# Mixers' recurrence: the pairwise key-query products in column quarters and halves of TensorE

## The chip, the cores and the metric

The kernel runs on one core of a Trainium2 chip. The metric is the device time of one execution in microseconds; lower is better. The profile is that of one profiled execution.

## The reference, cut to what matters

The program is a block with four mixers and experts, and behind it a block of two hybrid layers. The change lies in the hybrid layers, in the gated recurrence that runs over the sequence once forwards and once backwards:

```python
def hgrn2_chunk_scan(q, k, v, g):
    ...
        diff = bt[:, :, :, None, :] - bt[:, :, None, :, :]
        dec = jnp.where(mask, jnp.exp(jnp.where(mask, diff, 0.0)), 0.0)
        attn = jnp.einsum('bhtk,bhtsk->bhts', qt, dec * kt[:, :, None, :, :])
        o_intra = jnp.einsum('bhts,bhsv->bhtv', attn, vt)
...
    g_f = hgrn_log_forget(...)
    g_b = hgrn_log_forget(...)
    o_fwd = hgrn2_chunk_scan(hq, -jnp.expm1(g_f), hv, g_f)
    o_bwd = jnp.flip(hgrn2_chunk_scan(jnp.flip(hq, 1), jnp.flip(-jnp.expm1(g_b), 1),
                                      jnp.flip(hv, 1), jnp.flip(g_b, 1)), 1)
```

There are 512 tokens, four heads of width 128 and two layers. For each pair of a query token t and a key token s not behind it, `attn` is a sum over 128 channels of query times key times the decay between the two.

## The kernel before

**Tiling.** In the kernel a chunk is 128 tokens, so there are four chunks (`NT`) and four heads (`H`). The decay between s and t has no form that is safe over 128 tokens in one product, so `attn` of a chunk is put together in six rounds. `round0` makes the pairs that lie within the same four tokens. `level(d, i)`, with i from 1 to 5, makes the pairs that lie in the two halves of a block of 8, 16, 32, 64 and 128 tokens: in each block one half holds the queries, the other the keys (`half_of(i)` is 4, 8, 16, 32, 64). `d` is 0 for the forward direction and 1 for the backward one.

**Before the change** each of these products is made for all 128 keys of a chunk at once: 16 products in a round (four chunks, four heads), each with a 128x128 operand of keys as weights and with 128 query columns (`round0`) or 64 (`level`) as input. The result, 128 keys by the queries, goes to PSUM (`L`, named `lev` in the rows, four banks). Most of it is of no use, since a key of one block is never paired with a query of another. VectorE then copies only the wanted pairs under a mask into `att` (`keep0`, `keep`: L3865 and L3878, COPY_PREDICATED). Operands are plain float32; the profile shows two passes (LDWEIGHTS and MATMUL) for each such product, 32 passes a round. Transposes (L3175) and the fp32r products of the projection take one pass each.

**Order.** Each engine has its program written out by hand, with semaphores between them. TensorE puts a weight tile of the input projection (`tile(n)`: 24 passes of 128x512, L3138, L3139, L3144) behind each round, so the order forwards is `round0(0)`, `turn_values(0)`, `tile(10)`, `level(0,1)`, `turn_values(1)`, `tile(11)` and so on to `level(0,5)`, `tile(15)`, then `turn_keys`. Backwards it is `tile(20)`, `round0(1)`, `level(1,1)`, `rot(1)`, `tile(21)`, `level(1,2)`, `rot(2)`, `tile(22)` and so on. `rot(i)` (L3247) is the rotation for the attention's positions.

**What waits for what.** `round0` waits for `weigh0` (VectorE, L3849 and L3850, semaphore `decayed`). `level(d,i)` waits for `weigh(d,i)` (L3857, L3858) and for the masked copies that free its two banks (`kept`). VectorE's steps are, for each level, `low_part(n)` (L3779: the low half of a weight tile, which waits for the product of tile n-2), `far` (L3842, L3843), `weigh`, `keep` and, backwards, `rope` (L3918 to L3921). ScalarE takes the projections out of PSUM (L3513), splits the weights (L3503) and makes the exponentials (L3537). `rot(i)` waits until `rope(i-1)` has read its bank. `to_end(d)` (L3884, L3885) waits for level 4.

Of the kernel before, what the change touches and what calls it, by code (L numbers as in the profile page):

```python
# [14 lines left out]
P = 128  # L15
# [151 lines left out]
@contextmanager  # L167
def stage(nc, *names):

    with ExitStack() as ctx:  # L170
        sems = [ctx.enter_context(nc.semaphore(n)) for n in names]
        with nc.Block() as block:
            yield (block, *sems)
        nc.clear_and_free_semaphores(sems)
        nc.all_engine_barrier()
# [180 lines left out]
def parts_of(K, x, n=S):  # L356

    with ExitStack() as ctx:
# [6 lines left out]
NORM_SEMS = ["x_mean", "x_centred", "x_squared", "x_var", "x_root", "x_inverse", "x_spread", "x_scaled", "x_biased",  # L365
             "x_high", "x_low"]


EARLY_SEMS = ["e_summed", "e_shift", "e_prepared", "e_centred", "e_squared"]
# [2577 lines left out]
def mixers(K, a, layer, x, cs, sn, gain, bias):  # L2947
# [5 lines left out]
    nc = K.nc  # L2953
    lam_init = 0.8 - 0.6 * float(np.exp(-0.3 * layer))
    share = 1.0 - lam_init
    with ExitStack() as ctx:
# [6 lines left out]
        with ExitStack() as c1:  # L2963
# [28 lines left out]
            L = K.ps(c1, "lev", [P, 4, 512])  # L2992
# [5 lines left out]
            z = [quad["z0"], quad["z1"], quad["z2"]]  # L2998
# [50 lines left out]
            def half_of(i):  # L3049
                return 4 << (i - 1)  # L3050

            def query_side(ap, i, d):

                return ap.rearrange("p g (n two m) -> p g n two m", two=2, m=half_of(i))[:, :, :, 0 if d else 1, :]
# [6 lines left out]
            def blocks(t, m):  # L3061
# [7 lines left out]
                     "a_gathered", "a_summed", "a_stored", "m_scored", "m_max", "m_exps", "m_mixed", "m_turned", "m_gathered",  # L3069
                     "m_summed", "m_stored", "d_squared", "d_mean", "d_root", "d_normed",  # L3070
                     "mv_turned", "mv_taken", "yh_ready", "yl_ready", "eps_ready", "w_taken", "positions_in",
                     "turned", "rope_ready"] + EARLY_SEMS + NORM_SEMS
            with stage(nc, *names) as (block, *sems):
                (loaded0, loaded1, loaded2, mem_in, high_ready, low_ready, product, taken, lam_prod, lam_sum,
                 lam_exp, own, lb_diff, lb_ready, gate_in, clamped, logs, k_ready, q_ready, offset, decay,
# [3 lines left out]
                 a_gathered, a_summed, a_stored, m_scored, m_max, m_exps, m_mixed, m_turned, m_gathered,  # L3079
                 m_summed, m_stored, d_squared, d_mean, d_root, d_normed,  # L3080
                 mv_turned, mv_taken, yh_ready, yl_ready, eps_ready, w_taken, positions_in,
                 turned, rope_ready), norm_sems = sems[:-len(NORM_SEMS) - len(EARLY_SEMS)], sems[-len(NORM_SEMS):]
                early = Early(K, x, 6, K.mu[:, :], K.spare[:, :], lambda j: kk[j // 4][:, j % 4, :], sems[-len(NORM_SEMS) - len(EARLY_SEMS):-len(NORM_SEMS)])
                norm = Norm(K, x, gain, bias, X0[:, :], X1[:, :], lambda j: xsq[j // 4][:, j % 4, :], turned_t[:, 0:P],
                            norm_sems, high, low)
# [38 lines left out]
                def _(pe):  # L3124
# [52 lines left out]

                    def round0(d):
                        pe.wait_ge(decayed, 14 * d + 2)
                        if d:  # L3180
                            pe.wait_ge(state_ready, 3)
                            pe.wait_ge(put_f, 4)
                        for c in range(NT):
                            s = slice(c * P, (c + 1) * P)
                            for h in range(H):
                                mm = nc.tensor.matmul(L[:, c, h * P:(h + 1) * P], z[1][:, h, s], z[0][:, h, s], start=True, stop=True)
                            mm.then_inc(matched, 1)

                    def level(d, i):
                        zz = z[(i + 1) % 3]  # L3190
                        zq = query_side(zz[:, :, :], i, d)
                        n64 = 64 // half_of(i)
                        pe.wait_ge(decayed, 14 * d + 2 + 2 * i)
                        pe.wait_ge(kept, 14 * d + (4 if i < 3 else 2 * i))
                        for j in (0, 1):
                            for cc in (0, 1):
                                c = 2 * j + cc
                                for h in range(H):
                                    g = (cc * H + h) * 64
                                    mm = nc.tensor.matmul(L[:, 2 * (i % 2) + j, g:g + 64], zz[:, h, c * P:(c + 1) * P],  # L3200
                                                          zq[:, h, c * n64:(c + 1) * n64, :], start=True, stop=True)
                            mm.then_inc(matched, 1)

                    def turn_keys(d, h):
# [210 lines left out]
                    for n in range(FIRST_TILES, 10):  # L3415
                        tile(n)
                    round0(0)
                    turn_values(0)
                    tile(10)
                    for i in range(1, 6):  # L3420
                        level(0, i)
                        if i < 4:
                            turn_values(i)
                        tile(10 + i)
# [9 lines left out]
                    rot(0)  # L3434
                    tile(20)
                    round0(1)
                    for i in range(1, 6):
                        level(1, i)
                        rot(i)
                        tile(20 + i)  # L3440
# [330 lines left out]
                def _(dve):  # L3771
                    step = Own(dve, own)

                    def low_part(n):
                        if n >= given:
                            dve.wait_ge(high_ready, n + 1 - given)
                        if n >= 2:
                            dve.wait_ge(product, n - 1)
                        nc.vector.tensor_tensor(wl[:, n % 2, 0:unit_width(n)], raw_of(n), high_of(n), ALU.subtract).then_inc(low_ready, 1)  # L3779
# [20 lines left out]
                    def clamp(d):  # L3800
                        if d:
                            dve.wait_ge(gate_in, 1)
                            dve.wait_ge(k_turned, 4)
                            dve.wait_ge(decay, 10)
                        else:
                            dve.wait_ge(taken, 4)
                        if layer:
                            dve.wait_ge(lb_ready, 1)
                            for h in range(H):
                                step.go(nc.vector.tensor_scalar(kk[d][:, h, :], kk[d][:, h, :], lb[:, 1, d, h:h + 1], lb[:, 0, d, h:h + 1],  # L3810
                                                                ALU.mult, ALU.add))
                            step.all()
                        nc.vector.tensor_scalar(b[:, :, :], kk[d][:, :, :], 2.0 ** -60, None, ALU.max).then_inc(clamped, 1)
                        nc.vector.tensor_scalar(z[2][:, :, :], kk[d][:, :, :], 1e-20, 2.0 ** -60, ALU.max, ALU.min).then_inc(clamped, 1)
# [188 lines left out]
                        rope_quarter()  # L4003
                    low_part(5)
                    clamp(0)
                    dve.wait_ge(lam_exp, 1)
                    step(nc.vector.tensor_tensor(neglam[:, 0:1], neglam[:, 1:2], neglam[:, 0:1], ALU.subtract))
                    step(nc.vector.tensor_scalar(neglam[:, 0:1], neglam[:, 0:1], lam_init, None, ALU.subtract))
# [389 lines left out]
def second_block(K, a, x, out):  # L4398
    with ExitStack() as ctx:
        cs = K.sb(ctx, "cs", [P, S])  # L4400
        sn = K.sb(ctx, "sn", [P, S])
        K.spare = K.ps(ctx, "x_var", [P, S])
        for layer in range(2):
            first = (lambda t: K.col("ln_in_g_2", t), lambda t: K.col("ln_in_b_2", t))
            later = (lambda t: K.col("ln2_g_2", t), lambda t: K.col("ln2_b_2", t))
            mixers(K, a, layer, x, cs, sn, *(later if layer else first))
            feed_forward(K, a, layer, x, lambda t: K.col("ln1_g_2", 8 * layer + t), lambda t: K.col("ln1_b_2", 8 * layer + t))
        last_norm(K, x, lambda t: K.col("ln2_g_2", 8 + t), lambda t: K.col("ln2_b_2", 8 + t), out)
# [73 lines left out]
```

## Time and profile before

| | us |
|---|---|
| time, median of 3 runs | 3530.47 |
| lowest and highest run | 3528.61, 3533.96 |
| span of the profiled execution | 3526.3 |
| TensorE (PE) busy in it | 3363.8, 95% |
| VectorE (DVE) busy | 2510.4, 71% |
| ScalarE (ACT) busy | 1906.0, 54% |

The profiled execution's own time outside its span is not recorded; the median of the runs lies 4.2 us above the span. The whole program has 45471 instructions. The two hybrid layers' mixers lie at about 1834 to 2290 us and 2690 to 3135 us of the span; the six rounds of the forward direction in the first of them start at 1909.28 us, those of the backward direction at 2005.13 us. TensorE matmuls are pipelined, so the duration of one is longer than the distance to the next; the distances between starts are what counts.

### The profile page before, as it was taken

To read this page: it belongs to the slowest core of one execution; us is meant where nothing else is said; L and a number is where in the kernel's file an instruction comes from. 1 tells how busy PE (TensorE), PEld (TensorE's weight loads), DVE (VectorE), ACT (ScalarE), POOL (GpSimd) and SP (SyncE) were. 2 spreads that over 40 slices of the span, in tenths; PEclk is the share of its full clock that TensorE was granted. 3 is DMA by queue.
4 is the path that set the end of the run, shared out by engine and by line. 5 is a ranking of instruction groups with operands and counts; after the bars stand their busy time and mean duration, and the time that the engine had idled before them with its cause. 6 is when DMAs were issued, how large, how long until landed. Compare 5 with 4: busy or idle time off the path is not lost. (4 is left out here: it accounts for less than half of the span.)

```text
span 3526.3 us, 45471 instructions
## 1 busy us (share of the span) xinstructions
PE 3363.8 (95%) x16942; PEld 2708.0 (77%) x16942; DVE 2510.4 (71%) x2900; ACT 1906.0 (54%) x2152; POOL 241.4 (7%) x202
## 2 busy tenths in 40 slices
PE   8998987999999999999989998999999999899998
PEld 6886665888888888888758886778887887678886
DVE  6654566999999999999757766566536775656543
ACT  4223334778777877778646536344415534534422
POOL 0000000122121212121100000000000000000000
PEclk9998997999999999999979999999999999999999
DMA  4110236999999999999812110223331111023331
GB/s 151 49 31 27 64 117 238 363 367 368 365 370 363 369 364 369 369 368 367 291 39 84 60 61 29 68 84 96 107 97 65 62 55 59 24 86 96 97 108 65
DMA packets 118802, 600.28 MB, mean 170 GB/s; under 512 B 20722, under 2 KB 24194, under 8 KB 68130
## 3 DMA queue, kind: packets, MB, share of 16 engines
q1 hardware_dynamic: 105346, 580.93, 45.4%
q0 software_dynamic: 13312, 17.35, 2.0%
q8 instruction: 100, 1.64, 0.2%
q14 instruction: 44, 0.36, 0.0%
HBM read 586.06 MB, written 28.90 MB: 174 GB/s over the span
## 5 line engine op out<-in xcount | busy, mean ns | idle before, releaser
L2486 DVE TENSOR_TENSOR wl<-raw,wh 128x2048 fp32r<-128x2048 f32 x384 | 872.7, 2286 | 52.0 <-ACT wh L2415 52.0
L2415 ACT ACTIVATE wh<-raw 128x2048 fp32r<-128x2048 f32 x384 | 735.6, 1916 | 189.0 <-PE pu L2360 144.4
L2358 PE MATMUL pu<-wh,Xh 128*128 128x512 f32 x1024 | 409.7, 400 | 0.0
L2360 PE MATMUL pu<-wh,Xl 128*128 128x512 f32 x1024 | 399.9, 391 | 0.0
L2359 PE MATMUL pu<-wl,Xh 128*128 128x512 f32 x1024 | 399.8, 390 | 0.0
L4300 ACT ACTIVATE w_high<-w_raw 128x1024 fp32r<-128x1024 f32 (+1 forms) x114 | 131.3, 1151 | 320.4 <-PE acc L4272 161.1
L4347 DVE TENSOR_TENSOR w_low<-w_raw,w_high 128x1024 fp32r<-128x1024 f32 (+1 forms) x114 | 152.4, 1337 | 185.3 <-PE ps L4230 100.0
L4252 PE MATMUL ps<-x_high,w_high 128*128 128x512 f32 x656 | 255.2, 389 | 0.0
L4253 PE MATMUL ps<-x_low,w_high 128*128 128x512 f32 x656 | 255.2, 389 | 0.0
L2358 PEld LDWEIGHTS pu<-wh,Xh 128*128 128x128 f32 x1024 | 192.7, 188 | 45.4 <-issue 8.1
L2360 PEld LDWEIGHTS pu<-wh,Xl 128*128 128x128 f32 x1024 | 192.6, 188 | 42.0
L2359 PEld LDWEIGHTS pu<-wl,Xh 128*128 128x128 f32 x1024 | 193.0, 188 | 37.2
L3138 PE MATMUL acc<-x_high,w_high 128*128 128x512 f32 x528 | 218.5, 414 | 1.5 <-ACT hq L3513 1.5
L2358 PE MATMUL pd<-wh,hh 128*128 128x512 f32 x512 | 208.8, 408 | 0.2 <-DVE hl L2500 0.2
L3139 PE MATMUL acc<-x_low,w_high 128*128 128x512 f32 x528 | 207.6, 393 | 0.0
L2360 PE MATMUL pd<-wh,hl 128*128 128x512 f32 x512 | 200.3, 391 | 0.0
L2359 PE MATMUL pd<-wl,hh 128*128 128x512 f32 x512 | 199.6, 390 | 0.0
L4230 PE MATMUL ps<-x_high,w_low 128*128 128x512 f32 x704 | 173.2, 389 | 0.0
L3779 DVE TENSOR_TENSOR w_low<-w_raw,w_high 128x1024 fp32r<-128x1024 f32 (+1 forms) x102 | 115.6, 1135 | 57.9 <-PE acc L3144 28.3
L4230 PEld LDWEIGHTS ps<-x_high,w_low 128*128 128x128 f32 x704 | 132.1, 188 | 27.4
L4252 PEld LDWEIGHTS ps<-x_high,w_high 128*128 128x128 f32 x656 | 123.1, 188 | 25.6
L4253 PEld LDWEIGHTS ps<-x_low,w_high 128*128 128x128 f32 x656 | 123.1, 188 | 25.5
(784 smaller groups left out, 6837.8 us busy)
## 6 DMA issues: line engine op xcount, KB each, us to landing
raw<-in_exp_w SPq DMA_DIRECT2D x384, 1024.0 KB, 7.6
w_raw<-in_w_in SPq DMA_DIRECT2D x100, 512.0 KB, 3.4
w_raw<-in_w_up SPq DMA_DIRECT2D x82, 512.0 KB, 3.8
w_raw<-in_w_down SPq DMA_DIRECT2D x32, 704.0 KB, 4.0
w_raw<-in_w_out SPq DMA_DIRECT2D x32, 384.0 KB, 3.1
kv_raw<-in_w_mem_kv SPq DMA_DIRECT2D x16, 512.0 KB, 3.7
x<-in_x SPq DMA_DIRECT2D x4, 1024.0 KB, 8.2
w_raw<-in_w_out SPq DMA_DIRECT2D x8, 512.0 KB, 4.9
```

What stands on the lines that cost most here:

```text
L2358: nc.tensor.matmul(o, lh[:, k, :], wh[:, m % PARTS, c], start=(m >= 8 and kh == 0 and kk == 0), stop=False)
L2359: nc.tensor.matmul(o, lh[:, k, :], wl[:, m % PARTS, c], start=False, stop=False)
L2360: mm = nc.tensor.matmul(o, ll[:, k, :], wh[:, m % PARTS, c], start=False, stop=end)
L2415: nc.scalar.activation(wh[:, m % PARTS, :], raw[:, m % RAW, :], ACT.Copy).then_inc(w_high, 1)
L2486: nc.vector.tensor_tensor(wl[:, m % PARTS, :], raw[:, m % RAW, :], wh[:, m % PARTS, :], ALU.subtract).then_inc(w_low, 1)
L3138: nc.tensor.matmul(o, wh[:, n % 3, c], high[:, k, :], start=(k == 0), stop=False)
L3139: nc.tensor.matmul(o, wh[:, n % 3, c], low[:, k, :], start=False, stop=False)
L4230: mm = nc.tensor.matmul(o, wl[:, u % 2, c], high[:, k, :], start=False, stop=(k == DT - 1))
L4252: nc.tensor.matmul(o, wh(u)[:, c], high[:, k, :], start=(k == 0), stop=False)
L4253: nc.tensor.matmul(o, wh(u)[:, c], low[:, k, :], start=False, stop=False)
L4300: nc.scalar.activation(wh(u), raw_of(u), ACT.Copy).then_inc(high_ready, 1)
L4347: nc.vector.tensor_tensor(wl[:, u % 2, 0:width(u)], raw_of(u), wh(u), ALU.subtract).then_inc(low_ready, 1)
```

## The change

Only the part of each product that is used is made. In `round0` and in levels 1 to 3 no pair crosses a block of 32 tokens, so each product becomes four: 32 keys as weights (a 128x32 operand) by the 32 queries (`round0`) or 16 (levels 1 to 3) of the same 32 tokens. The result of a quarter goes to partitions r to r+32 of the bank, which puts the quarter on a quarter of TensorE's columns. Level 4 makes two products of 32 keys, one for each block of 64. Level 5 makes one of 64 keys. Each direction so has 4 x 64 + 32 + 16 = 304 products where it had 96, which is 832 more in the program. What these products no longer write is still read under the mask, so VectorE once clears three of the banks ahead of the first round (`lev_cleared`), and `round0` waits for that too. The masked copies are as before.

```diff
                     def round0(d):
                         pe.wait_ge(decayed, 14 * d + 2)
+                        pe.wait_ge(lev_cleared, 1)
...
                         for c in range(NT):
-                            s = slice(c * P, (c + 1) * P)
                             for h in range(H):
-                                mm = nc.tensor.matmul(L[:, c, h * P:(h + 1) * P], z[1][:, h, s], z[0][:, h, s], start=True, stop=True)
+                                for r in (0, 32, 64, 96):
+                                    s, g = slice(c * P + r, c * P + r + 32), h * P + r
+                                    mm = nc.tensor.matmul(L[r:r + 32, c, g:g + 32], z[1][:, h, s], z[0][:, h, s], start=True, stop=True)
                             mm.then_inc(matched, 1)
                     def level(d, i):
...
-                                    mm = nc.tensor.matmul(L[:, 2 * (i % 2) + j, g:g + 64], zz[:, h, c * P:(c + 1) * P],
-                                                          zq[:, h, c * n64:(c + 1) * n64, :], start=True, stop=True)
+                                    if i == 5:
+                                        r = 64 * d
+                                        mm = nc.tensor.matmul(L[r:r + 64, 2 * (i % 2) + j, g:g + 64], zz[:, h, c * P + r:c * P + r + 64],
+                                                              zq[:, h, c:c + 1, :], start=True, stop=True)
+                                        continue
+                                    if i == 4:
+                                        for side in (0, 1):
+                                            r = 64 * side + 32 * d
+                                            mm = nc.tensor.matmul(L[r:r + 32, 2 * (i % 2) + j, g + 32 * side:g + 32 * side + 32],
+                                                                  zz[:, h, c * P + r:c * P + r + 32], zq[:, h, c * n64 + side:c * n64 + side + 1, :],
+                                                                  start=True, stop=True)
+                                        continue
+                                    for part in range(4):
+                                        r, b0 = 32 * part, c * n64 + part * n64 // 4
+                                        mm = nc.tensor.matmul(L[r:r + 32, 2 * (i % 2) + j, g + 16 * part:g + 16 * part + 16],
+                                                              zz[:, h, c * P + r:c * P + r + 32], zq[:, h, b0:b0 + n64 // 4, :],
+                                                              start=True, stop=True)
...
                     clamp(0)
+                    nc.vector.memset(L[:, 0:3, :], 0.0).then_inc(lev_cleared, 1)
                     dve.wait_ge(lam_exp, 1)
```

On TensorE, at `round0(0)` and `level(0,1)` in the first layer, the instructions stand so (the size is that of the result; `z` are the weighted keys and queries):

```order
 L3144 MATMUL acc<-x_high,w_low 128x512 x8
-L3186 MATMUL lev<-z_168,z_169 128x128 x16
+L3188 MATMUL lev<-z_168,z_169 32x32 x64
 L3175 MATMUL x_mu<-const,hout 128x128 x4
 L3138 MATMUL acc<-x_high,w_high 128x512
```

```order
-L3200 MATMUL lev<-z_170 128x64 x16
+L3216 MATMUL lev<-z_170 32x16 x64
 L3175 MATMUL x_mu<-const,hout 128x128 x4
```

The rounds stay where they were; only their number of products and the tile of TensorE that each uses change.

At `level(0,4)` and `level(0,5)`, again on TensorE:

```order
-L3200 MATMUL lev<-z_170 128x64 x16
+L3210 MATMUL lev<-z_170 32x32 x32
 L3138 MATMUL acc<-x_high,w_high 128x512
```

```order
-L3200 MATMUL lev<-z_168 128x64 x16
+L3204 MATMUL lev<-z_168 64x64 x16
 L3138 MATMUL acc<-x_high,w_high 128x512
```

Here too a projection tile follows directly.

On VectorE one instruction is added, in the setup of the recurrence, between `clamp(0)` (the two rows ahead of it) and the two small steps on `neglam`:

```order
+L3830 TENSOR_SCALAR sums<-hff 128x2048
+L3831 TENSOR_SCALAR z_170<-hff 128x2048
+L4023 MEMSET lev 128x1536
+L4025 TENSOR_TENSOR neglam<-neglam 128x1
+L4026 TENSOR_SCALAR neglam<-neglam 128x1
+L3796 TENSOR_TENSOR w_low<-w_raw,w_high 128x1024
```

Nothing else moved on VectorE, and nothing on ScalarE, GpSimd or the DMA queues.

## Rows read from the trace of the kernel before

**Rows 1.** The page's part 1: busy time of each engine.

```profile
PE 3363.8 (95%) x16942; PEld 2708.0 (77%) x16942; DVE 2510.4 (71%) x2900; ACT 1906.0 (54%) x2152; POOL 241.4 (7%) x202
```

**Rows 2.** Windows: stretch, its length; busy PE, PEld, DVE, ACT, POOL; PE clock, DMA.

```profile
1918.80:1928.20 9.40, 9.40 (x61) 8.45 (x60) 9.40 (x11) 3.95 (x4) 0.00 (x0) 1.00 0.34 112
1937.70:1947.10 9.40, 9.40 (x61) 8.45 (x60) 5.53 (x6) 3.95 (x4) 0.00 (x0) 1.00 0.19 56
2025.00:2035.00 10.00, 10.00 (x61) 8.52 (x59) 9.93 (x12) 3.46 (x3) 0.00 (x0) 1.00 0.15 53
```

**Rows 3.** Timeline, PE, forward rounds: start, us, instructions merged.

```profile
1909.28 3.73 PE L3186 MATMUL lev<-z,z 128*128 128x128 f32 x32
1912.85 0.60 PE L3175 MATMUL x_mu<-const,hout 128*128 128x128 f32 x4
...
1947.12 3.68 PE L3200 MATMUL lev<-z 128*128 128x64 f32 x32
1950.61 0.48 PE L3138 MATMUL acc<-x_high,w_high 128*128 128x512 f32 x1
```

**Rows 4.** Timeline, PE, products with 32 columns of weights, and their neighbours.

```profile
2092.47 0.60 PE L3258 MATMUL x_mu<-const,dv 128*128 128x128 f32 x4
2093.00 1.08 PE L3263 MATMUL lev<-z,const 128*32 128x128 f32 x32
2094.01 0.50 PE L3138 MATMUL acc<-x_high,w_high 128*128 128x512 f32 x1
...
2666.62 1.74 PE L428 MATMUL x_var<-sq,const 128*32 128x128 f32 x56
```

**Rows 5.** Timeline, PE, products with 64 columns of weights and 64 of input.

```profile
279.13 0.34 PE L1574 MATMUL G<-x,btt 128*64 128x64 f32 x4
...
279.53 0.33 PE L1575 MATMUL G<-vt,ktt 128*64 128x64 f32 x4
```

**Rows 6.** Instructions that touch `lev`: weight loads, ns min/median/max.

```profile
L3200 PEld LDWEIGHTS lev<-z x640: 186/192/338, 1918.6 to 2887.9; 128*128 128x128 f32 x160
...
L3263 PEld LDWEIGHTS lev<-z,const x64: 106/110/110, 2093.0 to 2928.9; 128*32 128x32 f32 x64
```

**Rows 7.** Groups of DVE, 1909 to 1965 us (busy, mean ns, waits); then timeline.

```profile
L3878 DVE COPY_PREDICATED att<-const,lev 128x512 f32<-128x512 int32 x8 | 5.7, 722 | 7.8 <-PE lev L3200 7.8
...
1959.86 2.29 DVE L3889 TENSOR_TENSOR z<-hff,z 128x2048 f32<-128x2048 f32 x1 [4.89 <-ACT ends L3546]
```

**Rows 8.** Timeline, DVE, backward rounds.

```profile
2032.79 1.22 DVE L3779 TENSOR_TENSOR w_low<-w_raw,w_high 128x1024 fp32r<-128x1024 f32 x1
...
2037.34 1.22 DVE L3858 TENSOR_TENSOR z<-hfb,z 128x1024 f32<-128x1024 f32 x1
...
2041.74 1.22 DVE L3779 TENSOR_TENSOR w_low<-w_raw,w_high 128x1024 fp32r<-128x1024 f32 x1
...
2050.88 1.23 DVE L3779 TENSOR_TENSOR w_low<-w_raw,w_high 128x1024 fp32r<-128x1024 f32 x1 [5.64 <-PE acc L3144]
```

**Rows 9.** Timeline, PE, backward rounds.

```profile
2010.88 3.76 PE L3200 MATMUL lev<-z 128*128 128x64 f32 x32 [2.02 <-DVE att L3865]
...
2040.69 3.68 PE L3200 MATMUL lev<-z 128*128 128x64 f32 x32
2044.20 1.08 PE L3247 MATMUL x_var<-dk,const 128*128 128x512 f32 x2
2048.79 1.98 PE L3144 MATMUL acc<-x_high,w_low 128*128 128x512 f32 x8
...
2056.35 1.10 PE L3247 MATMUL x_var<-dk,const 128*128 128x512 f32 x2 [2.06 <-DVE rope_t L3918]
```

**Rows 10.** Timeline, DVE: where the clearing goes, and a copy out of PSUM.

```profile
1879.71 0.16 DVE L4007 TENSOR_TENSOR neglam<-neglam 128x1 f32<-128x1 f32 x1 [3.18 <-ACT neglam L3642]
...
2072.73 0.68 DVE L3899 COPY hfb<-lev 128x512 f32<-128x512 f32 x1
```

**Rows 11.** Windows, second layer, backward: columns as in rows 2.

```profile
2845.00:2850.00 5.00, 5.00 (x15) 3.68 (x16) 4.97 (x5) 2.88 (x4) 0.00 (x0) 0.50 0.32 105
```

More of the change, by code:

```diff
@@ L3071, in mixers @@
                      "mv_turned", "mv_taken", "yh_ready", "yl_ready", "eps_ready", "w_taken", "positions_in",
-                     "turned", "rope_ready"] + EARLY_SEMS + NORM_SEMS
+                     "turned", "rope_ready", "lev_cleared"] + EARLY_SEMS + NORM_SEMS
             with stage(nc, *names) as (block, *sems):
@@ L3081, in mixers @@
                  mv_turned, mv_taken, yh_ready, yl_ready, eps_ready, w_taken, positions_in,
-                 turned, rope_ready), norm_sems = sems[:-len(NORM_SEMS) - len(EARLY_SEMS)], sems[-len(NORM_SEMS):]
+                 turned, rope_ready, lev_cleared), norm_sems = sems[:-len(NORM_SEMS) - len(EARLY_SEMS)], sems[-len(NORM_SEMS):]
                 early = Early(K, x, 6, K.mu[:, :], K.spare[:, :], lambda j: kk[j // 4][:, j % 4, :], sems[-len(NORM_SEMS) - len(EARLY_SEMS):-len(NORM_SEMS)])
```

## Prediction

> **What bounds the kernel now.** I read the busy shares first, then windows over the forward and backward rounds, and then the timeline of each engine there. TensorE is busy 95% of the span [rows 1], but a share over the whole span says nothing of these rounds. In the windows it is busy without a gap in the forward rounds (9.40 of 9.40 us), while VectorE is full in the first of them (9.40 of 9.40) and has room later (5.53 of 9.40) [rows 2]. In the backward rounds both are full: TensorE 10.00 of 10.00, VectorE 9.93 [rows 2]. So forwards a shorter round ends the stage earlier; backwards it does so only until VectorE is the bound. The second layer repeats the pattern.
>
> A round costs what its weight loads cost. `round0` takes from 1909.28 to 1912.85, 3.57 us for 32 passes; a level takes from 1947.12 to 1950.61, 3.49 us [rows 3]. That is 110 ns a pass whether 128 or 64 columns are fed in, so it is not the input that sets it.
>
> **What a pass costs after the change.** No row before shows 32 columns of weights with 32 columns of input. The nearest are the products of `h_means` (32 columns of weights, 128 of input, put in turn on the four quarters): 32 passes, whose last starts 1.08 less one pass's 0.27 = 0.81 us after the first, 26 ns a pass; and a run of 56 of the same kind, (1.74 - 0.27)/55 = 27 ns [rows 4]. For one quarter that is a pass every 4 x 27 = 108 ns, the time that 128 input columns take, so four quarters work at the same time, and each is held by its input. A weight load of 32 columns takes 110 ns where one of 128 takes 192 [rows 6]: 82 ns less for 96 columns, 0.85 ns a column, 27 ns for 32. With 32 columns of input, or 16, a quarter then needs 27 ns a pass plus whatever does not overlap. How much that is, the products with 64 by 64 show: two halves, eight passes each, all 16 started within 0.51 us (279.13 to 279.53 + 0.33 - 0.22) [rows 5], so 73 ns a step against 0.85 x 64 = 54 ns. Scaled by the same 1.35, a quarter needs 37 ns, and four of them give a pass every 9 ns. I take 10 ns; the floor is 27/4 = 7 ns, the ceiling that a row gives is 27 ns.
>
> **Changing the tile costs too.** The last full-width product ahead of `h_means` starts at 2092.47 + 3 x 0.11 = 2092.80 and the first narrow one at 2093.00, 0.20 us later instead of 0.11; behind the last one (2093.81) the next full one starts at 2094.01, again 0.20, and takes 0.50 instead of 0.39 since its weights were not loaded ahead [rows 4]. I take 0.09 + 0.03 going in and 0.17 + 0.11 coming out: 0.4 us a round.
>
> **The sum, forwards.** Before: 3.57 + 5 x 3.49 = 21.0 us. After: `round0` and levels 1 to 3 have 4 x 128 passes at 10 ns, 5.1 us; level 4 has 64 passes on two quarters, 37/2 = 18.5 ns each, 1.2; level 5 has 32 passes that all fall on one half, 73 ns each, 2.3; six tile changes 2.4. Together 11.0 us, so 10.0 less. Can the others follow? VectorE waited 7.8 us for these rounds and then 4.89 us on ScalarE's exponentials [rows 7]; those stand behind ScalarE's copy of `tile(14)`, which comes earlier with TensorE. 12.7 us of slack hold 10.0 of gain. If only the 7.8 could be used, 2.2 us a layer would be missing.
>
> **The sum, backwards.** VectorE needs 2041.74 - 2032.79 = 8.95 us a level [rows 8], and TensorE about 9.9: `level(1,4)` starts at 2040.69 though its operand was there at 2037.34 + 1.22 = 2038.56 [rows 8, 9]. VectorE cannot be made faster by this, so all that TensorE saves in `round0` and levels 1 to 3, beyond these 2.1 us, turns into waits. Then level 4 itself: it would start at 2038.56, take 1.2 + 0.4, and `rot(4)` would start at 2040.16 instead of 2044.20, 4.0 us earlier; `tile(24)` behind it ends 4.0 us earlier too (before: 2048.79 + 1.98), and that is what VectorE waited 5.64 us for at 2050.88 [rows 8, 9]. Level 5 is hidden: `rot(5)` waits for VectorE afterwards in any case (2.06 us) [rows 9]. So 4.0 us.
>
> **Added work at no cost.** The clearing writes 128x1536. A copy of 128x512 out of the same banks takes 0.68 us [rows 10], so at most three times that, 2.0 us. It falls between `clamp(0)` and the step on `neglam`, where VectorE waits 3.18 us for ScalarE [rows 10]. Without that cover it would cost 2.0 us a layer. Behind it stand the `neglam` steps and `low_part(6)`, which start no later. `round0`'s added wait is long met: the clearing lies over 29 us ahead of it (1879.71 against 1909.28) [rows 3, 10]. No DMA and no queue is moved; the weight tiles are asked for by `low_part`, so earlier along with the rest.
>
> A layer gains 10.0 + 4.0 = 14.0 us, two 28.0. The profiled span would go from 3526.3 to 3498.3, and with the 4.2 us between span and median, 3530.5 becomes 3502.5. I say **3502 us**.
>
> With 7 ns a pass (13.5 and 54 ns for levels 4 and 5) it is 12.4 + 4.3 a layer, 3497; with no cost of changing tiles either, 2.8 us a layer more, 3491. The other bound follows as a rival.
>
> **Rivals.**
>
> *A pass has a price of its own.* Nothing shows a long run of passes closer than 27 ns, and the input of 128 columns explains that as well as a fixed price would. At 27 ns a quartered round costs 128 x 0.027 + 0.4 = 3.9 us and loses 0.4; level 4 costs 2.1, level 5 2.7. Forwards 21.0 - 20.2 = 0.8 us are gained, backwards 1.4 at level 4; 2.2 a layer, 3526, which a measurement cannot tell from no change. For it: four times as many instructions for TensorE's sequencer, 208 products more in each direction. Against it: within a group of four the narrow products start far closer together, or 32 passes with four quarters each busy 108 ns could not fit into 0.81 us [rows 4]. The Trainium skill speaks for it ("TensorEngine Tiling (Array Packing)", section Instruction Overhead): each matmul has an overhead of about 60 cycles, so that one with a single column of input is as slow as one with 60. By that page's figure, 25 ns a pass, an estimate gives 1.8 + 1.5 us a layer and 3524. Whether the figure holds for passes on different quarters no row here shows.
>
> *Slower: the quarters do not overlap in this order.* The two passes of a product go to the same quarter. If the second holds up all that stands behind it, weight load and input of each pass come in a row, 27 + 27 = 54 ns a pass, 6.9 + 0.4 us a round. Forwards that is 4 x 3.8 + 0.4 - 0.8 = 14.8 us more, and backwards TensorE becomes the bound again with some 13 us more: 28 a layer, 3586. The sign turns near 28 ns a pass (forwards 576 passes against 21.0 - 2.4 - 2.3 = 16.3 us). Against it: `h_means` has two passes a product in the same order and overlapped [rows 4].
>
> *The clock.* In the second layer TensorE's granted clock was at half, 1.2 GHz, from 2845 to 2850 [rows 11], close behind the place where in the first layer it waited 2.02 us for the masked copies of `keep0` [rows 9]. VectorE ends `keep0` no earlier relative to `round0(1)`, so this wait grows to about 2.02 + 3.57 - 1.7 = 3.9 us, and each backward level gets one near 1 us. A half clock over 7 us costs 3.5 us of work, in both layers and perhaps twice: 3506 to 3516.
>
> *VectorE binds forwards as well*, since it is full until 1928 [rows 2]: then only the 7.8 us of its waits come back, less what is late to reach it, some 10 a layer: 3510.
>
> **How the numbers follow.** As forecast 0.55 (its own range 3495 to 3509), clock 0.13, VectorE forwards 0.10, a price of 12 to 20 ns a pass 0.06 (about 3508 to 3518), fixed price 27 ns 0.08, slower 0.08. About 0.2% or 7 us is what a measurement of this kernel can tell from no change, so all but the last two are faster, with a little of each neighbour: faster 0.83, same 0.09, slower 0.08. The range runs from 3493 to 3522.
>
> **What would show it.** In the changed kernel's timeline `round0` should span 1.2 to 1.6 us to the next full product instead of 3.57, level 4 1.6, level 5 2.5 to 2.7; the first row behind a round should be long (0.50). `turn_keys(0)` should follow `round0(0)` 10 us sooner. Backwards the levels should begin with waits for VectorE near 1 us, and its step should stay at 8.95. The clearing should stand inside the wait for `neglam`. The prediction is wrong if a quartered round takes over 2.5 us, if the wait at `keep0(1)` is followed by a long stretch of half clock, or if VectorE's forward waits vanish while it still sets the end.

## The result, and the profile after

The changed kernel takes 3495.45 us (median of 4 runs, 3490.97 to 3506.21), the kernel before 3529.54 us beside it. The ratio is 0.9904, with a 95% interval of 0.9884 to 0.9924: 34 us faster, where 28 were forecast. The profiled execution's span went from 3526.3 to 3493.1 us.

Engines by busy time, after (page, part 1; before in [rows 1]):

```profile
PE 3319.5 (95%) x18606; PEld 2652.5 (76%) x18606; DVE 2511.9 (72%) x2902; ACT 1905.6 (55%) x2152; POOL 240.7 (7%) x202
```

TensorE has 44 us less to do, and is at 95% still. The forward rounds of the first layer, TensorE's timeline (start, duration, instructions merged; source lines behind the change are up to 18 further on):

```profile
1908.20 1.98 PE L3144 MATMUL acc<-x_high,w_low 128*128 128x512 f32 x8
1910.10 1.35 PE L3188 MATMUL lev<-z,z 128*32 128x32 f32 x128
1911.38 0.66 PE L3175 MATMUL x_mu<-const,hout 128*128 128x128 f32 x4
...
1917.44 1.30 PE L3216 MATMUL lev<-z 128*32 128x16 f32 x128
...
1939.34 1.21 PE L3210 MATMUL lev<-z 128*32 128x32 f32 x64
1940.48 0.50 PE L3138 MATMUL acc<-x_high,w_high 128*128 128x512 f32 x1
...
1946.14 2.08 PE L3204 MATMUL lev<-z 128*64 128x64 f32 x32
1948.15 0.50 PE L3138 MATMUL acc<-x_high,w_high 128*128 128x512 f32 x1
...
1953.73 1.03 PE L3231 MATMUL lev<-const,z 128*128 128x128 f32 x8
```

Against [rows 3] `round0` goes from 3.57 to 1.28 us (1910.10 to 1911.38), level 5 from 3.49 to 2.01, level 4 to 1.14, and levels 1 to 3, of which the first is shown, to 1.23 each. From `round0(0)` to `turn_keys(0)` it is 43.6 us in place of 56.0.

Backwards, TensorE, first layer; then VectorE. `round0(1)` starts at 1993.70.

```profile
1999.37 1.91 PE L3216 MATMUL lev<-z 128*32 128x16 f32 x128 [4.32 <-DVE att L3882]
2002.21 2.05 PE L3264 MATMUL x_var<-dq,const 128*128 128x512 f32 x2 [0.93 <-DVE rope_t L3935]
...
2027.09 1.21 PE L3210 MATMUL lev<-z 128*32 128x32 f32 x64 [0.17 <-DVE z L3875]
2029.04 1.10 PE L3264 MATMUL x_var<-dk,const 128*128 128x512 f32 x2 [0.74 <-DVE rope_t L3935]
...
2041.17 1.36 PE L3264 MATMUL x_var<-dk,const 128*128 128x512 f32 x2 [3.58 <-DVE rope_t L3935]
```

```profile
2012.34 1.23 DVE L3796 TENSOR_TENSOR w_low<-w_raw,w_high 128x1024 fp32r<-128x1024 f32 x1
...
2021.27 1.23 DVE L3796 TENSOR_TENSOR w_low<-w_raw,w_high 128x1024 fp32r<-128x1024 f32 x1
...
2035.69 1.22 DVE L3796 TENSOR_TENSOR w_low<-w_raw,w_high 128x1024 fp32r<-128x1024 f32 x1 [1.95 <-PE acc L3144]
```

VectorE's step is 8.93 us, as before [rows 8], its wait of 5.64 us is down to 1.95, and TensorE now waits for VectorE, 4.32 us for `keep0(1)` where it was 2.02 [rows 9]. The windows show what the clock did (stretch, length; busy PE, PEld, DVE, ACT, POOL; TensorE's granted clock; DMA share, GB/s); first after, then the second layer of before:

```profile
1998.00:2008.00 10.00, 7.70 (x140) 5.81 (x141) 9.93 (x13) 4.39 (x4) 0.00 (x0) 0.51 0.30 99
2038.00:2048.00 10.00, 6.83 (x21) 5.04 (x22) 9.71 (x10) 2.02 (x2) 0.00 (x0) 0.83 0.13 49
```

```profile
2838.00:2848.00 10.00, 7.96 (x49) 7.28 (x47) 9.93 (x13) 3.34 (x3) 0.00 (x0) 0.77 0.17 57
2848.00:2858.00 10.00, 10.00 (x55) 8.31 (x54) 9.35 (x11) 3.46 (x3) 0.00 (x0) 0.89 0.22 66
```

A mean of 0.51 is the lower level, 1.2 GHz, nearly throughout; 0.83 is a third of the stretch at it (10 x 0.17/0.5 = 3.4 us). The first window after lies behind the wait for `keep0(1)`, the second behind the 3.58 us wait at `rot(5)`. Before, in its second layer, 4.6 + 2.2 = 6.8 us at the lower level lie behind its own wait for `keep0(1)`, and another stretch lies behind the wait at `rot(5)`. In its first layer there is none in either place. TensorE and its windows, before, second layer:

```profile
2890.27 1.21 PE L3247 MATMUL x_var<-dk,const 128*128 128x512 f32 x2 [2.07 <-DVE rope_t L3918]
...
2899.14 1.04 PE L3214 MATMUL lev<-const,z 128*128 128x128 f32 x8
```

```profile
2890.00:2895.00 5.00, 4.73 (x12) 3.45 (x13) 4.74 (x5) 1.57 (x2) 0.00 (x0) 0.66 0.02 3
```

This second stretch is 5 x 0.34/0.5 = 3.4 us long.

Where the time went, between the first starts of the named operations in the timelines (us):

| kernel | forwards: `round0(0)` to `turn_keys(0)`, layers 1, 2 | backwards: `round0(1)` to `turn_keys(1)`, layers 1, 2 |
|---|---|---|
| before | 55.96, 55.96 | 58.92, 63.39 |
| after | 43.63, 43.61 | 56.35, 56.29 |
| e1, change forwards only | 43.59, 43.59 | 63.42, 64.99 |
| e2, change backwards only | 55.97, 55.96 | 56.39, 56.31 |
| e3, rounds 0 to 3 only | 47.23, 47.23 | 59.11, 58.03 |
| e4, quarters in a row | 52.41, 52.41 | 63.79, 62.66 |
| e5, products twice | 59.11, 60.15 | 62.53, 68.87 |
| e6, clearing only | 55.96, 55.96 | 63.44, 63.39 |
| e7, half tile in the gap | 43.59, 43.59 | 56.71, 56.25 |
| e8, reordered | 43.63, 43.68 | 51.31, 51.34 |
| e9, before with the half tile | 55.96, 55.96 | 59.03, 63.48 |
| e10, `round0` thrice | 53.01, 54.35 | 60.97, 61.09 |
| e11, the change again | 43.62, 43.63 | 56.37, 56.24 |
| e12, reordered again | 43.59, 43.59 | 51.34, 51.34 |

Forwards 12.3 us a layer are gained, backwards 2.6 and 7.1; together 34.4, against 34.1 between the medians and 33.2 between the two profiled spans.

### The profile page after: what moved, and what is told of

It reads as the page before. It is cut to its first block and busy times, and to the rows that moved or that the text cites. A ratio compares the mean times of both kernels' runs of the same rounds, so it can differ in the third digit from the quotient of the medians.

```text
span 3493.1 us, 48805 instructions
## 1 busy us (share of the span) xinstructions
PE 3319.5 (95%) x18606; PEld 2652.5 (76%) x18606; DVE 2511.9 (72%) x2902; ACT 1905.6 (55%) x2152; POOL 240.7 (7%) x202
```

## The experiments

**Which direction gives what (e1, e2).** The products of the other direction are whole, as in:

```diff
+                                if d == 1:
+                                    s = slice(c * P, (c + 1) * P)
+                                    mm = nc.tensor.matmul(L[:, c, h * P:(h + 1) * P], z[1][:, h, s], z[0][:, h, s], start=True, stop=True)
+                                    continue
```

> The change in the forward direction alone; the backward products are whole. The traces of before and after put 12.3 and 12.4 us of the gain between the first forward round and the transposes of the keys. Theory (TensorE alone sets the end forwards, so each round gives all that it saves): 24.7 us faster than before, 3505. Rival (VectorE also binds forwards, as the prediction allowed): 20 us or less. Rival (part of what looks like a forward gain is lost again further on, where a wait takes it up): under 20 us. Backwards the wait behind keep0(1) should be 2.0 us, as before.

> The change in the backward direction alone. Theory (VectorE's step of 8.95 us bounds the levels, and the gain is the earlier start of rot(4) and tile(24)): 4 to 5 us a layer at most, 8 to 10 us in all, with keep0(1) followed by a gap of 4.3 us on TensorE and a stretch of half clock behind it. Rival (TensorE alone sets the end here too): all that the rounds save, about 12.4 us a layer, 25 in all. Rival (the clock's fall eats the gain): under 5 us in all. The whole change gave 34 us, of which 24.7 lie forwards, so 9.4 should be found here if the two parts add.

Forwards alone: 3511.13 us, 0.9946 of before (0.9931 to 0.9962), so 13 to 24 us faster, a little short of the 24.7. In the trace the forward stretch gives all of it (12.4 a layer), and the backward stretch was 4.5 and 1.6 us longer than in the trace of before. That looks like the last of the three stories (24.7 less 6.1 is 18.6 us), but it doesn't show it: e6, whose products are all whole, also took 63.4 us backwards in both layers, so it is the first layer of the trace of before, with its full clock, that stands apart. Why the second layer here took 65.0 us one trace can't tell. Why the median lies below 24.7 us stays open. Backwards alone: 3520.84, 0.9974 (0.9960 to 0.9989), 4 to 14 us, with 56.4 and 56.3 us backwards as after the whole change. By the ratios the parts add to 28 us, within their errors the 34 of the whole. That TensorE bounds the backward rounds, which would give 25 here, is refuted; that VectorE also binds forwards is refuted by the trace of e1.

**Which rounds (e3).** Levels 4 and 5 stay whole in both directions (`if i >= 4:` in front of the old product).

> Round 0 and levels 1 to 3 in quarters, levels 4 and 5 whole as before, both directions. By the sum of the traces: forwards 2.3 + 3 x 2.26 less 0.09 a round for entering, 8.7 us a layer; backwards only the 2.1 us by which TensorE was behind VectorE at level 4. Theory: 10.8 us a layer, 21.6 us faster than before, 3508. Rival (TensorE bounds backwards as well): 17 us a layer, 34 in all. Rival (levels 4 and 5 carry little, since one works on two quarters and the other on one half only): within 5 us of the whole change, over 29 us.

3507.83 us, 0.9933 (0.9916 to 0.9949): 24 us, as theory had it, against the 34 of a stage bounded by TensorE and the 29 if levels 4 and 5 carried little. The interval (18 to 30 us) just touches the 29; the trace rules it out, since levels 4 and 5 carry 47.23 - 43.6 = 3.6 us a layer forwards alone, 7.2 in all, over the 5 of that story. Forwards 8.73 us a layer, as worked out. Backwards the agreement is partly luck. TensorE, first layer:

```profile
1994.09 1.35 PE L3188 MATMUL lev<-z,z 128*32 128x32 f32 x128
...
2027.48 3.79 PE L3203 MATMUL lev<-z 128*128 128x64 f32 x32 [0.29 <-DVE z L3879]
2031.10 1.08 PE L3268 MATMUL x_var<-dk,const 128*128 128x512 f32 x2
```

`level(1,4)` starts 33.39 us behind `round0(1)` where before it was 35.56 (2005.13 to 2040.69, [rows 9]): the 2.1 us are there, 2.2 by these rows. But the keys came no sooner, 59.1 against 58.9 us, since behind it the clock was at half for part of the way:

```profile
2036.00:2048.00 12.00, 9.93 (x49) 7.96 (x48) 9.96 (x10) 3.56 (x4) 0.00 (x0) 0.75 0.14 44
```

**The clearing (e6).** Before, with the clearing and `round0`'s wait for it.

> The kernel before with the clearing of three banks and round0's wait for it alone. Theory (it lies inside the wait for neglam): 0 us, within 1 us of before. Rival (what stands behind it on VectorE is late by its 1.34 us): 2.7 us slower.

3528.94 us, 0.9996 (0.9981 to 1.0011). The median shows nothing; the interval alone doesn't exclude 2.7 us, so the place decides (VectorE's timeline):

```profile
1873.63 1.34 DVE L4007 MEMSET lev<- 128x1536 f32 x1 [0.32 <-issue]
1876.49 0.16 DVE L4009 TENSOR_TENSOR neglam<-neglam 128x1 f32<-128x1 f32 x1 [1.52 <-ACT neglam L3643]
```

It is followed by a wait of 1.52 us that was 3.18 [rows 10]: inside the cover. Apart from the clearing this is the kernel before once more, and it took 63.4 us backwards in both layers.

**The price of a pass (e4, e5).** e4 has the same products, with the loop over quarters outside the loop over heads:

```diff
-                            for h in range(H):
-                                for r in (0, 32, 64, 96):
+                            for r in (0, 32, 64, 96):
+                                for h in range(H):
```

> The same narrow products as in the change, but ordered so that 4 heads (round 0) or 8 products (levels) fall on one quarter in a row before the next quarter has its turn. Theory (each quarter needs about 35 ns a pass for itself, and only products on different quarters overlap): round 0 and levels 1 to 3 span 128 x 0.035 + 0.1, about 4.5 us, level 4 about 2.2 us, level 5 unchanged at 2.0; forwards 43.6 becomes 58, the backward levels are bounded by TensorE, and the whole is about 3540. Rival (the order does not matter, the sequencer sets 9 ns a pass): 1.3 us a round, 3495. Rival (weight load and input of a quarter come one after the other, 54 ns a pass): 6.9 us a round, over 3570.

```profile
1907.05 2.74 PE L3188 MATMUL lev<-z,z 128*32 128x32 f32 x128
1909.72 0.66 PE L3175 MATMUL x_mu<-const,hout 128*128 128x128 f32 x4
1915.79 3.53 PE L3212 MATMUL lev<-z 128*32 128x16 f32 x128
1919.25 0.66 PE L3175 MATMUL x_mu<-const,hout 128*128 128x128 f32 x4
```

3528.59 us, 0.9997 of before (0.9984 to 1.0010): in the time of the whole the same narrow products in this order give nothing that can be told from noise (at most 6 us), and not the 3540 us that theory said. In the trace the forward stretch is 52.41 us, 3.6 shorter than before, where theory had it at 58. `round0`, with 8 passes on a quarter in a row, spans 2.67 us, the levels, with 16, 3.46. Both rivals are out (1.3 and 6.9). With a price q for each pass and a saving s at each change of quarter (15 and 7 of them), 127q - 15s = 2.54 and 127q - 7s = 3.35 (each merged duration less the last pass's own 0.20 and 0.18) give q = 32 ns. Level 4, with 64 passes and three changes, wasn't used for this and agrees: 63q - 3s = 1.71, and its row reads 1.91, less 0.20 again 1.71. Theory's 35 was near, but it had forgotten s, 0.10 us, by which the next quarter starts early, and so put the round at 4.5. In the change a quarter has its turn every 4 x 9 ns = 36 ns ((1.35 - 0.20)/127 = 9 ns a pass). So it is the quarter's own 32 to 36 ns, shared by four; level 4 on two quarters gives (1.21 - 0.20)/63 = 16 ns, again 32.

e5 issues each product of round 0 and levels 1 to 3 twice (`for r in (0, 32, 64, 96, 0, 32, 64, 96)`).

> Each quartered product of round 0 and levels 1 to 3 is issued twice with the same result, 256 passes a round in place of 128; levels 4 and 5 as in the change. It measures the price of a pass without the change of tile. Theory (9 to 10 ns a pass): round 0 spans 2.45 to 2.6 us in place of 1.28; forwards 43.6 becomes about 48.4; backwards VectorE covers most of it, 0 to 2 us a layer; in all 10 to 13 us slower than the change. Rival (the price is in the change of tile, and a pass costs under 5 ns): round 0 under 1.9. Rival (the sequencer falls behind in a longer run, 20 ns a pass or more): over 3.8 us.

3543.26 us, 1.0045 (1.0025 to 1.0065), slower than before the change. Forwards 15.5 and 16.5 us a layer were added, not 4.8. TensorE at `round0(0)`:

```profile
1906.21 1.70 PE L3188 MATMUL lev<-z,z 128*32 128x32 f32 x171
1910.55 0.96 PE L3188 MATMUL lev<-z,z 128*32 128x32 f32 x85 [2.63 <-issue]
```

For 171 passes the pace is 9 ns ((1.70 - 0.20)/170), then TensorE does nothing for 2.6 us with no semaphore to wait for, and goes on at the old pace. The third story, a longer run falling behind, came true in another form than it was told: not a slower pace, but single stops. The four doubled rounds are 12.6 us longer in the first layer; the rest of the 15.5 lies in two stretches of half clock, 3.4 us each, behind such stops. The next kernel (e10) has `(0, 32, 64, 96) * 3`, in `round0` alone:

> Each product of round 0 is issued three times, 384 passes in a row; all else as in the change. With the products twice, passes started 8 to 9 ns apart except for single stalls (2.8 us behind pass 172 of round 0). Theory (instructions come in from memory more slowly than 9 ns a pass; a run is fed from what lies ready, and stalls once that is used up): in the first layer's round 0 a stall of 2 to 3 us behind pass 150 to 180, and another about 128 passes later; the round spans 7.5 to 10 us. Rival (the stalls come from two products writing the same place): the passes would wait all alike, no single long stall, and none at 172. Rival (the stall was chance): round 0 spans 3.4 us.

```profile
1904.28 1.67 PE L3188 MATMUL lev<-z,z 128*32 128x32 f32 x171
1908.25 1.31 PE L3188 MATMUL lev<-z,z 128*32 128x32 f32 x128 [2.30 <-issue]
1912.25 1.39 PE L3188 MATMUL lev<-z,z 128*32 128x32 f32 x85 [2.69 <-issue]
```

```profile
1905.80:1908.20 2.40, 0.15 (x17) 1.00 0.57 203
1908.20:1909.40 1.20, 1.15 (x128) 1.00 0.03 10
1909.40:1912.20 2.80, 0.16 (x19) 0.57 0.02 6
1912.20:1913.50 1.30, 1.25 (x85) 0.50 0.05 13
```

The stop comes behind pass 171 again, and the next exactly 128 passes later; one execution, 3520.48 us. The second fence is TensorE's windows over the stops, first and third row, and the passes behind them (busy time, clock, DMA share, GB/s): one stop falls into a time of much DMA traffic (0.57), the other of little (0.02), so the kernel's own transfers don't make them. Writing to one place twice doesn't either, which would show in each pass.

The 171 is no limit of its own. It belongs to the place of this round in the program: in the other `round0` of both kernels the first stop comes behind pass 197, 194 and 220. A short run isn't safe either. The rows below `...` are `level(1,1)`, 128 passes as in the change, 0.9 us behind the tripled `round0(1)` of the second layer, and it stops behind its pass 91 (the first row is the first part of that `round0(1)`):

```profile
2829.10 2.09 PE L3188 MATMUL lev<-z,z 128*32 128x32 f32 x220
...
2839.38 1.44 PE L3216 MATMUL lev<-z 128*32 128x16 f32 x91 [0.92 <-DVE att L3882]
2842.69 0.72 PE L3216 MATMUL lev<-z 128*32 128x16 f32 x37 [1.88 <-issue]
```

What all stops share is a distance: counted over TensorE's instructions of the trace (a pass is two, its weight load and its matmul; the few that wait or signal count too), every stop of e5 and e10 lies a multiple of 256 behind the one before it, within one. And the page has a DMA queue that carries instructions; here in the change, in e10 and in e5 (packets, MB, share of the engines):

```profile
q8 instruction: 113, 1.85, 0.2%
q8 instruction: 121, 1.98, 0.2%
q8 instruction: 129, 2.11, 0.2%
```

e10 has 2048 instructions more than the change and 8 transfers more, e5 has 4096 and 16: one transfer of 16 KB for 256 instructions. In the DMA records each of the 26 stops (over 0.1 us) ends 0.9 to 1.6 us behind the landing of such a transfer; for the second stop of e10 it runs from 1909.86 to 1910.79, and the passes go on at 1912.25. So instructions reach TensorE in portions of 256, that is 128 passes, and the stops are its waits for the next portion. In the long run of e10 a portion is used up in 1.2 us and the next resumption is 4.0 us behind the last (1908.25 to 1912.25), 31 ns a pass on the average. What keeps the transfers that far apart no row shows. None of the change's 24 rounds stops; behind each of its runs of 128 passes stands a tile, whose passes start 227 ns apart, or a wait for VectorE.

**The clock and the waits backwards (e7, e9, e8, e12).** In e7 half of `tile(21)` fills the wait for `keep0(1)`, and e9 does the same to the kernel before:

```diff
                     for i in range(1, 6):
+                        if i == 1:
+                            tile(21, 0)
                         level(1, i)
                         rot(i)
-                        tile(20 + i)
+                        tile(20 + i, 1 if i == 1 else None)
```

> The change, and half of tile(21) (12 passes, about 2.7 us) put between round0(1) and level(1,1), where TensorE waits 4.3 us for keep0(1). Clock theory (the gap brings the half clock from 1997 us on): the gap falls to 1.6 us, the half clock is gone or shorter. VectorE theory (it sets the levels backwards, the half clock is hidden): keys of the backward direction come at most 1.95 us sooner, since only VectorE's wait ahead of low_part(26) can go: 54.4 to 56.3 us from round0(1) in place of 56.3; in all 0 to 4 us faster than the change. Rival (the clock costs time here): 3 us a layer or more.

> The kernel before, with half of tile(21) between round0(1) and level(1,1), where its TensorE waits 2.0 us for keep0(1). From round0(1) to the keys of the backward direction the kernel before took 58.9 us in one layer of its trace, where the clock stayed full, and 63.4 in the other and in both layers of the run with the clearing alone, where the clock was at half for 6.8 us behind that wait. Clock theory (a wait of 2 us there brings the half clock in most layers of the kernel before, and that makes most of the difference between 7.1 us gained backwards and the 2.6 read from the first layer): no half clock in this stretch and 57 to 59 us in both layers, the whole 5 to 10 us faster than before. Rival (the half clock comes whether TensorE waits here or not): 63 us, no gain.

e7: 3498.30 us, 0.9905 (0.9891 to 0.9919), no better than the change, as the VectorE theory had it. TensorE, first layer:

```profile
2005.04 1.28 PE L3216 MATMUL lev<-z 128*32 128x16 f32 x128 [1.38 <-DVE att L3884]
2007.88 1.10 PE L3264 MATMUL x_var<-dq,const 128*128 128x512 f32 x2 [1.55 <-DVE rope_t L3937]
2014.91 1.30 PE L3216 MATMUL lev<-z 128*32 128x16 f32 x128 [3.17 <-DVE z L3877]
```

The wait was not removed but moved to the next rounds, as it must where VectorE sets the pace, and the half clock came behind the 3.17 us. e9: 3533.24 us, ratio 1.0000 (0.9987 to 1.0012). There too the wait turned up elsewhere:

```profile
2018.90 3.79 PE L3200 MATMUL lev<-z 128*128 128x64 f32 x32 [2.01 <-DVE z L3860]
```

and one layer kept its full clock (59.0 us), the other not (63.5), as in the trace of before. So the expectation failed, and e9 doesn't settle what decides whether the clock falls behind a wait of 2.0 us: over before, e1, e6 and e9, eight such layers, it fell in six. Whether filling the wait helps is thus not shown either way. What the half clock costs is settled: where TensorE sets the pace, as before the change, the stretch is 4.5 us longer with it, or 6.1 in e1's second layer, where the first stretch of it lasts 10.3 us and not 6.8. The 4.5 are two parts. `rot(5)` starts 54.53 us behind `round0(1)` in the second layer (2835.74 to 2890.27) and 51.22 in the first [rows 9], 3.3 later; the keys follow it by 8.87 us in place of 7.70, 1.2 more, and that is the second stretch of half clock, behind the wait at `rot(5)`. It came in the same six layers and in neither of the other two.

e8 also takes `tile(25)` ahead of `rot(5)`, where TensorE waited 3.58 us, and `rot(6)` behind `tile(26)`:

```diff
                         level(1, i)
+                        if i == 5:
+                            tile(25)
                         rot(i)
...
-                    rot(6)
                     for h in range(H):
                         turn_keys(1, h)
                     tile(26)
+                    rot(6)
                     contributions(1)
```

> As the half tile in the gap, and besides tile(25) ahead of rot(5) (where TensorE waits 3.58 us for VectorE's rope(4)), and rot(6) behind tile(26). If the waits that the change left behind are what still costs time, transposes of the keys come at 51 to 52 us from round0(1) in place of 56.3, and with the tile now ahead of them the stretch from round0(1) to h_means shortens by 3 to 5 us a layer: 3486 to 3490. If VectorE's own chain sets the end of the stage, it shortens by under 1.5 us a layer.

> The change itself once more, to stand beside the reordered version on one chip: 3495, ratio to before 0.988 to 0.992.

> The reordered version once more, beside the change: its stage is 4.2 us a layer shorter (51.3 + 29.9 us against 56.3 + 29.1 from round0(1) to h_means), so 8 us faster than the change, 0.2%: about 3487.

e8: 3490.20 us, 0.9891 (0.9874 to 0.9908). Beside each other on one chip the change took 3497.19 us (0.9900, 0.9882 to 0.9918; 3496.67 to 3502.66) and the reordered version 3488.59 (0.9871, 0.9851 to 0.9892; 3484.46 to 3490.51): 8.6 us faster, with no run in common, and the fastest kernel here. In its trace (e12) the only wait left in place of the 3.58 us is

```profile
2041.80 1.09 PE L3231 MATMUL lev<-const,z 128*128 128x128 f32 x8 [0.82 <-DVE z L3911]
```

and the stretch is 5.0 us shorter, of which 0.8 is given back between the keys and `h_means`. As e7 alone gave nothing, it comes from the two further moves; which of them gives how much no run separates.

## Why the prediction was right, and where its sizes were off

**The bound forwards** was right: no wait appears on TensorE in these rounds, and what the rounds save arrives at `turn_keys(0)`. **The sum forwards** was 2.3 us a layer too small, 10.0 for 12.3, in two terms. The passes, forecast at 5.1 + 1.2 + 2.3 = 8.6 us, took 1.15 + 3 x 1.12 + 1.01 + 1.86 = 7.4 (each merged duration less the last pass's own 0.18 to 0.22), at 9, 16 and 60 ns a pass for 10, 18.5 and 73. The changes of tile, forecast at 2.4, took the rest of the 8.66 us that now lie in the rounds (the spans above, 8.12, and six times 0.09 for entering: 1.90 us from the last tile row to `round0`, 1.81 before), so 1.3. The 0.4 a round that was taken from `h_means` was almost twice too high; perhaps since its last narrow pass has 128 input columns where these have 16 to 64, which no run tells apart.

**The price of a pass** by scaling rows 5 was 10 ns, measured 9; that only passes on different quarters overlap was shown by e4. The fixed price of 27 ns is refuted. So is, for this case, the Trainium skill's rule ("TensorEngine Tiling (Array Packing)", section Instruction Overhead) of about 60 cycles a matmul, where it is taken as a distance between any two passes: passes on four quarters start 9 ns apart. For passes on one quarter the 32 ns of e4 don't contradict it. But e5 and e10 show a limit of another kind, near 30 ns a pass on the average of a long run, set by the portions in which instructions arrive, which the prediction did not have.

**The sum backwards**, 4.0 us, was right up to `rot(5)`: `level(1,4)` starts 33.39 us behind `round0(1)` for 35.56, `rot(4)` 35.34 for 39.07, and VectorE's step on `w_low` 41.99 for 45.75, 3.8 us sooner. At the keys 2.6 are left in the first layer. The 1.2 us between are the 3.4 us of half clock behind the 3.58 us wait, in `tile(25)`. In the second layer it is 7.1: the same 3.8, and 3.3 more, which the kernel before lost there to the half clock behind `keep0(1)` and the changed one doesn't, since VectorE sets its pace; the 1.2 us behind `rot(5)` both kernels pay there. So the 4.0 a layer was right as a mechanism, and that 9.7 in all came near the forecast 8.0 is partly luck, as 1.2 were lost in one layer and 3.3 won in the other. The step that was off is the reading of the first layer of one trace as the rule: it is the exception, two of eight layers.

**The clock rival** came true in its mechanism and not in its price: the wait at `keep0(1)` grew to 4.32 us (3.9 was forecast), the clock fell behind it in both layers, and VectorE's step stayed at 8.93 us all the while, with no wait on VectorE until 2035.69. TensorE had the room. So the prediction's own sign of being wrong, a long stretch of half clock behind that wait, appeared (about 10 us of it in the first layer), and did not make it wrong. The half clock that was feared for the changed kernel was already a cost of the one before. The change hides the part behind `keep0(1)`; the part behind `rot(5)` it doesn't hide, 1.2 us a layer. **VectorE forwards** did not bind, but it is near: it ran without any wait through these rounds, and its operand for `level(0,2)` was there 1.5 us before TensorE took it (1923.2, 1924.7). **The clearing** took 1.34 us, under its bound of 2.0, inside the wait. **The slower rival** (54 ns, no overlap) was out: even in a row a quarter needs 32.

So the forecast was 6.4 us low (34.4 by the table, 28.0 forecast): 4.7 forwards and 7.1 + 2.6 - 8.0 = 1.7 backwards.

## What to carry to other kernels

Narrow products pay on TensorE above all when neighbours in the order go to different column quarters: the same products took 1.23 to 1.28 us a round in turn and 2.67 to 3.46 us in a row, where the whole ones took 3.5. Level 5, all on one half, still went from 3.49 to 2.01. Keep such passes apart by slower work: each 128 of them use up a portion of instructions, in 1.2 us at full pace, and the next came only about 4 us behind the last in a long run. One round of 128 passes with a tile behind it never stopped; 256 and more in a row nearly always did, and so did a round of 128 close behind them. Before costing a stage from one layer of one trace, read the granted clock in every repetition of it, and once an engine has been relieved, move its work into the waits that are left rather than filling one of them: here that gave 8.6 us more, and half a tile in one gap nothing.

## What was unexpected of the hardware

- TensorE ran 171 passes of 32 columns at 9 ns each and then stopped for 2.3 to 2.6 us without a semaphore to wait for; the next stop came 128 passes later. Such stops lie multiples of 256 TensorE instructions apart, last up to 3.3 us, and each ends 0.9 to 1.6 us behind a 16 KB transfer on the queue that carries instructions.
- In e10 the granted clock was full up to the second stop (1.00 in the window ahead of it) and then fell to the lower level, 1.2 GHz: 0.57 over the stop, 0.50 in the passes behind it.
- The number of input columns hardly counts below 32: on four quarters in turn passes with 16 started (1.30 - 0.18)/127 = 8.8 ns apart, those with 32 9.1. On a half, 64 by 64, (2.08 - 0.22)/31 = 60 ns.
